# Quarter-form steps for small experts, the first of them ahead of the second half of the gather, and another order of the expert pairs

## The reference

```
logits = h @ w_router;  top_val, top_idx = top_k(logits, 2);  gate = softmax(top_val)
y[t] = sum over the token's 2 experts e of gate * (silu(h[t] @ w_gate[e]) * (h[t] @ w_up[e])) @ w_down[e]
x = x + gate_f * y;  out = rmsnorm(x, g_final)
```

## Time and profile before

| what | value |
|---|---|
| median of 3 runs | 1672.86 us (1670.66 to 1673.17) |
| profiled execution | 1672.14 us |
| its span | 1670.4 us |
| TensorE busy | 1544.0 us (92%) |
| VectorE, ScalarE busy | 418.1 us, 250.2 us |
| DMA moved | 484.43 MB, mean 290 GB/s |
| mean granted TensorE clock | 0.969 |

### The profile page before, as it was taken

The page is one execution under the profiler, slowest core; times in us unless marked ns, Lnnn a source line. Parts: engine busy times, 40 slices in busy tenths (PEclk is TensorE's granted clock), DMA queues, the critical chain, the costliest instruction groups (busy, mean ns, idle before and its releaser), DMA issues.

```text
span 1670.4 us, 21757 instructions
## 1 busy us (share of the span) xinstructions
PE 1544.0 (92%) x8696; PEld 852.4 (51%) x8697; DVE 418.1 (25%) x955; ACT 250.2 (15%) x560; POOL 0.2 (0%) x4
## 2 busy tenths in 40 slices
PE   5988889999989998599999999999999999999996
PEld 2777658777657774444444443443333443333332
DVE  2366525333344533600002000110000300003003
ACT  2132210000012331110101010011111111111112
POOL 0000000000000000000000000000000000000000
PEclk8999799999999998799999999999999999999998
DMA  9974525765656440068979797999999999997991
GB/s 348 380 266 164 189 101 192 273 252 202 227 193 229 172 178 16 1 264 332 407 289 407 284 408 294 408 374 405 408 407 407 407 377 407 407 408 296 367 377 78
DMA packets 168185, 484.43 MB, mean 290 GB/s; under 512 B 10024, under 2 KB 20544, under 8 KB 168000
## 3 DMA queue, kind: packets, MB, share of 16 engines
q1 hardware_dynamic: 168128, 483.70, 75.8%
HBM read 482.63 MB, written 1.05 MB: 290 GB/s over the span
## 4 chain that ended last, share of the span: by engine, by line
PE 79%; DMA 9%; DVE 5%; SPq 3%; ACT 2%; issue 2%; DVEq 0%; ACTq 0%
PE bank L1024 11%; PE bank L931 9%; PE bank L1064 8%; DMA ring<-in_w_exp_up 8%; PE bank L778 7%; PE bank L1008 6%; PE bank L1185 6%; PE bank L1020 5%; PE bank L949 4%; PE bank L912 4%; PE bank L1058 3%; PE bank L1211 3%; PE bank L772 3%; SPq L629 2%; PE bank L1280 2%
## 5 line engine op out<-in xcount | busy, mean ns | idle before, releaser
L1024 PE MATMUL bank<-ring,hT 128*64 128x448 f32 x1280 | 255.1, 546 | 32.2 <-DMA ring<-in_w_exp_up 12.7
L1024 PEld LDWEIGHTS bank<-ring,hT 128*64 128x64 f32 x1280 | 89.0, 137 | 190.7 <-issue 153.7
L931 PE MATMUL bank<-hT,ring 128*128 128x256 f32 x704 | 158.0, 385 | 1.7 <-DVE hT L1429 1.7
L778 PE MATMUL bank<-hT,ring 128*128 128x256 f32 x640 | 153.0, 396 | 3.9 <-ACT hT L1953 2.5
L1809 DVE TENSOR_TENSOR bt<-arena,bank 64x512 f32<-64x512 f32 (+2 forms) x36 | 24.3, 675 | 493.5 <-PE bank L1024 249.6
L931 PEld LDWEIGHTS bank<-hT,ring 128*128 128x128 f32 x704 | 135.2, 193 | 24.1 <-issue 3.8
L778 PEld LDWEIGHTS bank<-hT,ring 128*128 128x128 f32 x640 | 124.5, 198 | 26.0 <-DVE hT L1429 4.4
L1064 PE MATMUL bank<-ring,bt 128*32 128x256 f32 (+1 forms) x1232 | 136.8, 445 | 0.0
L1348 DVE SCALAR_TENSOR_TENSOR acc<-ring,cond,acc 128x512 f32<-128x512 f32 x140 | 105.2, 752 | 4.9
L1020 PE MATMUL bank<-ring,hT 128*128 128x448 f32 x256 | 100.7, 546 | 4.1 <-DMA ring<-in_w_exp_up 3.4
L1008 PE MATMUL bank<-ring,hT 128*32 128x448 f32 x1024 | 102.8, 542 | 0.0
(11 more groups left out here) (279 smaller groups left out, 1179.8 us busy)
## 6 DMA issues: line engine op xcount, KB each, us to landing
ring<-in_w_exp_gate SPq DMA_DIRECT2D x128, 896.0 KB, 9.2
ring<-in_w_exp_up SPq DMA_DIRECT2D x128, 896.0 KB, 13.0
ring<-in_w_exp_down SPq DMA_DIRECT2D x64, 1536.0 KB, 15.9
ring<-in_w_ada SPq DMA_DIRECT2D x24, 2048.0 KB, 9.4
ring<-in_w_in SPq DMA_DIRECT2D x10, 2048.0 KB, 12.8
ring<-in_w_exp_down SPq DMA_DIRECT2D x32, 512.0 KB, 16.3
ring<-in_w_ff_gate SPq DMA_DIRECT2D x5, 2048.0 KB, 12.4
ring<-in_w_ff_up SPq DMA_DIRECT2D x5, 2048.0 KB, 12.8
```

Of the source, the lines that this page charges most:

```text
L778: last = mm(o[:, 0:T], w[:, k, t * P:(t + 1) * P], hT[:, k, :], start=(k == 0), stop=(k == KC - 1))
L931: last = mm(bank[n % 2][:, a * T:(a + 1) * T], w[a][:, k, t * P:(t + 1) * P], hT[:, k, :], start=(k == 0), stop=(k == KC - 1))
L1024: last = mm(o[64 * c2:64 * c2 + 64, 64 * c2:64 * c2 + EH], xsT[:, k, t0:t0 + 64], w[:, k, c2 * EH:(c2 + 1) * EH], start=(k == 0), stop=(k ...
```

## The change

- `TINY = 32` and class 0: an expert with at most 32 tokens takes `tiny_step`, which is the quarter form alone (8 rows k of four groups), one set of transposes, and the down product in quarter form into bank 7. It waits for a gate piece and an up piece together. With the counts above, experts 0, 5 and 7 are class 0 and expert 1 stays class 1.
- `STREAM_AT` and `LONE = 1`: ranks 5, 6, 7 take positions 6, 8, 2 (before: 2, 4, 6). Round 0 has experts 0, 4, 7; round 1 (J12 to J15) is the large expert 2 alone; round 2 (J16 to J23) pairs expert 1 with expert 3, round 3 (J24 to J31) expert 5 with expert 6.
- J0 runs ahead of the second gather half, which then goes to banks 4, 5, 6, 1; the clearing of bank 7 and J0's steps on VectorE and ScalarE move with it, and `stream_weights(0)` behind it. J0 no longer waits for `yacc`; J1 does.
- More tables and branches: the flag `has_small`, the class read in each iteration, and two forms of the copy of bank 7 into `ys`.

```diff
-STREAM_AT = (0, 1, 3, 5, 7, 2, 4, 6)
-LONE = 3
+STREAM_AT = (0, 1, 3, 5, 7, 6, 8, 2)
+LONE = 1
-        small_ = {0: 2 * (s_ // 2), 1: 4, 2: 6}.get(l_)
+        small_ = {0: 2 * (s_ // 2), 2: 6, 3: 8}.get(l_)
-JOBS_DONE = [12, 20, 28, 32]
+HAS_SMALL = [int(l_ != LONE and (l_, s_) != (0, 0)) for l_ in range(4) for s_ in range(ES)]
+JOBS_DONE = [12, 16, 24, 32]
+SECOND_BANKS = (4, 5, 6, 1)
+TINY = 32
...
+            def tiny_step(J, ends):
+
+                if ends is not None:
+                    pe.wait_ge(xsS_v, ends + 1)
+                    pe.wait_ge(yacc_v, 4 * ends + 12)
+                for k in range(0, KC, 2):
+                    pe.wait_ge(full_g[k // 2], 16 * J + 16)
+                    pe.wait_ge(full_u[k // 2], 16 * J + 16)
+                    quarter(TX, range(k, k + 2), True)
+                pe.wait_ge(yzS_v, 1 if ends is None else ends + 1)
+                pe.wait_ge(eh_v, 4 * J + 4)
+                h, one_ = hs[64:P, 0, :], ident[64:P, 64:P]
+                mm(bank[3][:, 0:64], h[:, 0:P], one_, start=True, stop=True)
+                for t in range(1, 4):
+                    last = nc.tensor.transpose(bank[3][:, t * 64:(t + 1) * 64], h[:, t * P:(t + 1) * P], one_)
+                last.then_inc(et_p, 4)
+                down(J, 0, 0, ALL, (0,), 7)
...
             with pe.If(misfit == 0):
+                tiny = class_at(pe, 0)
                 pe.wait_ge(xsS_v, 1)
-                turn_scatter_weights(0, bank[3])
+                with pe.If(tiny == 0):
+                    tiny_step(0, None)
+                with pe.Else():
+                    small_step(0, None)
+                gather(1, SECOND_BANKS)
+                turn_scatter_weights(0, bank[0])
+                pe.wait_ge(sgt_a, 1)
...
-                        with pe.If(l != LONE):
-                            small_step(J, ends)
+                        partner = has_small(pe, l, i)
+                        tiny = class_at(pe, 2 * ends)
+                        with pe.If(partner == 1):
+                            with pe.If(tiny == 0):
+                                tiny_step(J, ends)
+                            with pe.Else():
+                                small_step(J, ends)
...
             with ve.If(misfit == 0):
-                stream_weights(0)
+                tiny = class_at(ve, 0)
                 gathered(0)
                 small_window(None)
+                nc.vector.memset(bank[7][:, :], 0.0).then_inc(yzS_v, 1)
+                with ve.If(tiny == 0):
+                    stream_step(0, 0)
+                with ve.Else():
+                    stream_step(0, 1)
+                stream_weights(0)
                 gathered(1)
                 large_window(1)
-                ve.wait_ge(sgt_p, 1)
-                stream_weights(1)
                 signal(nc.vector.memset(ys, 0.0), dv)
                 nc.vector.tensor_copy(yacc, xs[:, :, :]).then_inc(yacc_v, 4 * NE + 1 - 20)
                 for i in (4, 5, 6):
                     last = nc.vector.memset(bank[i][:, :], 0.0)
                 last.then_inc(yzL_v, 1)
-                ve.wait_ge(sgt_a, 1)
-                nc.vector.memset(bank[7][:, :], 0.0).then_inc(yzS_v, 1)
+                ve.wait_ge(sgt_p, 1)
+                stream_weights(1)
```

More of the change, by code:

```diff
@@ L972, in _, with gather @@
             mm(bank[1][:, 2 * NE:3 * NE], ones, chosen[:, 1, :], start=False, stop=True).then_inc(r_p, 1)
-            for h in range(2):
+            def gather(h, banks):
                 pe.wait_ge(sel_v, 2 + h)
@@ L981, in _ @@
                         last.then_inc(gat_p, 1)
+            gather(0, range(4))
             def hidden(r, J, n, i, a, unit, c=0):
@@ L1002, in hidden, with quarter @@
                         last.then_inc((eg_p, eu_p)[a], 3 if n == 1 else before_last(n, i))
-            def quarter(t0, ks):
+            def quarter(t0, ks, alone=False):
                 for k in ks:
@@ L1011, in quarter @@
                             last.then_inc(u_used if q == 3 else g_used, 1)
+                        elif alone and k == KC - 2 and q % 2:
+                            last.then_inc(eu_p if q == 3 else eg_p, 3)
             def stream_hidden(J, n, i, a, t0, c=0):
@@ L1177, in up_parts @@
                 for part_, (lo, hi) in enumerate(((0, SPLIT), (SPLIT, EH))):
-                    if part_:
+                    if part_ and ends is not None:
                         pe.wait_ge(yacc_v, 4 * ends + 12)
@@ L1301, in _ @@
                         with pe.If(l == 0):
-                            small_step(J + 2, ends)
+                            with pe.If(tiny == 0):
+                                tiny_step(J + 2, ends)
+                            with pe.Else():
+                                small_step(J + 2, ends)
                             with pe.If(i == 1):
@@ L1306, in _ @@
             with pe.Else():
+                gather(1, range(4, 8))
                 with nc.Fori(0, NE, engines=PE, head_slot={PE[0]: 0}) as r:
@@ L1806, in stream_step @@
                     up_ready(J, n, i)
-                    rows_, o = (slice(64, P), bank[2]) if n > 1 and i == ITEMS[n] - 1 else (slice(0, P), bank[1])
+                    rows_, o = (slice(64, P), bank[2]) if n != 1 and i == ITEMS[n] - 1 else (slice(0, P), bank[1])
                     n_ = EH if n == 3 and i < 2 else CW
@@ L1831, in stream_end @@
                         large_out(2, jobs)
-                nc.vector.tensor_copy(ys[64:P, 1, CW:D], bank[7][64:P, :]).then_inc(ys_v, 1)
+                with ve.If(class_at(ve, 2 * g) == 0):
+                    for c in (2, 3):
+                        last = nc.vector.tensor_copy(ys[64:96, 1, c * T:(c + 1) * T], bank[7][32 * c:32 * c + 32, 0:T])
+                    last.then_inc(ys_v, 1)
+                with ve.Else():
+                    nc.vector.tensor_copy(ys[64:P, 1, CW:D], bank[7][64:P, :]).then_inc(ys_v, 1)
                 small_window(2 * g + 2)
@@ L1882, in _ @@
                         with ve.If(l == 0):
-                            stream_step(J + 2, 1)
+                            with ve.If(tiny == 0):
+                                stream_step(J + 2, 0)
+                            with ve.Else():
+                                stream_step(J + 2, 1)
                             with ve.If(i == 1):
@@ L2034, in _, with gathered @@
             act(gt[:, :, 1], gt[:, :, 0], ACT.Exp).then_inc(r_a, 1)
-            for h in range(2):
+            def gathered(h, banks):
                 for g in (1, 3):
@@ L2161, in stream_end @@
                         large_out(2, jobs)
-                act(ys[64:P, 1, 0:CW], bank[7][0:64, :], ACT.Copy).then_inc(ys_a, 1)
+                with ae.If(class_at(ae, 2 * g) == 0):
+                    for c in (0, 1):
+                        ins = act(ys[64:96, 1, c * T:(c + 1) * T], bank[7][32 * c:32 * c + 32, 0:T], ACT.Copy)
+                    ins.then_inc(ys_a, 1)
+                with ae.Else():
+                    act(ys[64:P, 1, 0:CW], bank[7][0:64, :], ACT.Copy).then_inc(ys_a, 1)
                 scatter_weights_in(g + 1, bank[7])
@@ L2167, in _ @@
             with ae.If(misfit == 0):
-                scatter_weights_in(0, bank[3])
+                tiny = class_at(ae, 0)
+                with ae.If(tiny == 0):
+                    stream_step(0, 0)
+                with ae.Else():
+                    stream_step(0, 1)
+                gathered(1, SECOND_BANKS)
+                scatter_weights_in(0, bank[0])
                 with ae.Fori(0, 4) as l:
@@ L2184, in _ @@
             with ae.Else():
+                gathered(1, range(4, 8))
                 with ae.Fori(0, NE) as r:
```

47 lines of the change are left out of this document (32 added, 15 removed).

## The result

The changed kernel takes **1928.34 us** (median of 4 runs, 1925.82 to 1929.39) against 1672.09: a ratio of 1.153, 95% interval 1.151 to 1.155. The forecast was 1659. The steps became shorter and the kernel 256 us slower.

A forecast was written before the change was run, and what follows sets the result against it. DMA was taken to bound pairs and round 0, TensorE the lone expert. Start and round 0 gave 3.3 us, J11 7.4, the order with a tiny J24 4.9, less 1.9 small costs: 1659 us, range 1648 to 1671.

The forecast's parts named there:

- Small costs on the path: Extra branch and copy at three round ends 1.0 us (bounds 0 and 9), plus 0.9 for low-clock scatter products.
- DMA sets the pairs and round 0: Pairs of small and class-2 large steps have period 54.1 us, DMA-bound round 0 iterations 92.7, whatever small steps cost.
- A tiny step takes 12.4 us: Each tiny step: quarter form, SiLU, transposes and down sum to 12.4 us, 7.4 less than the half form.
- The start, 2.8 us won: J0 ahead of the second gather half starts at 697.5; J1 starts at 725.2, cold, net 2.8 us earlier.
- the second rival: Gain mostly eaten: first passages of new code cost 3.2 us at J0, J1, J11, a round end; 1665 mid-range; chance 0.20.
- J11 saves 7.4, the job behind the last round end 4.7, J0 on the way to J1 7.4: Savings from tiny steps at J11, at J24 behind the last round end, and at J0 before J1, in us.
- The order is worth nearly nothing: Lone expert second, rounds 2 and 3 after it: the order alone gives 0.2 us.
- From J10 on: End of round 0: TensorE binds from J10, J11 saves its whole 7.4 us, next round's first job starts at 1077.1.
- J31's quarter form: Last pair of round 3: reached at 1615.8, after six DMA-bound periods of 54.1 us from J19.
- the end: From J31's quarter form to the span's end: work as before, 38.95 us.
- The clock rival: Tiny steps leave TensorE idle, class-3 gate releases run at 1.2 GHz: 1709 us fully cold, 1676 at a third; chance 0.08.

The follow-up runs named there:

- e1: The whole change with TensorE's loop made compact, each form of step held once, same work and order, against the kernel before: 1671.57 us, ratio 1.0007.
- e2: The kernel before with two more copies of the small step in TensorE's inner loop that never run (136 unused products): 1913.64 us, one run.
- e4: The changed kernel without the half form behind round 0's large step, which this input never runs: 1686.03 us, one run.
- e5: As e1, but J0 back behind both gather halves and the copy into yacc: 1665.58 us, 0.998 of the kernel before.
- e6: As e1 with TINY = 0, so all small experts take the half form: 1689.23 us, 1.0113 of the kernel before.
- e7: As e5, but the large expert without a partner last again: 1669.07 us, 0.999 of the kernel before.
- e9: As e5, but the class-3 step does the quarter form's first six rows k between rows of the second up item: 1667.04 us, 0.9975 of before.

## Why the prediction was wrong

**The step that failed** is "Small costs on the path": 1.0 us, with bounds 0 and 9, where 257 us were measured (the changed kernel less e1). It priced one more branch at 0.37 us, a row of VectorE, and 3 us where code is passed for the first time, both per place and once. TensorE's loop, which grew by 128 products and transpositions, has no term in the sum. The mechanism left out is that the added code is part of a loop. The earlier trace rows did show such a wait (3.17 us of issue before J2), and I read it as a price of first passages that goes away. It went away in the old kernel, which fetches 3 packets from 840 us on. With some 530 instructions more in the body it does not: the price is paid in every pass, before nearly every step. e2 shows that unused code does this without any of the change, e1 and e4 that the change is rid of it with the same or nearly the same work.

What a page states would have pointed there: the Trainium skill, "Runtime: NRT & Kernel Launch", section "Instruction fetch mechanics", gives TensorE an instruction memory of 2048 instructions, refilled in 16 KiB blocks of 256 instructions, and says that a taken branch whose target lies outside the current window of two blocks has to wait for a fetch. The packets of 16.4 KB agree, and so do the packets inside the waits. The limit measured here, between 1745 and 1817, is below the stated size; seven of the page's blocks (1792) would fit it, which is an estimate from the page's figure. The window of two blocks does not agree with a body of 1745 instructions, full of jumps, that fetches next to nothing again.

The other steps can be judged on e1, where the code fits. Its chain of waits:

```profile
725.78 4.50 issue
730.28 20.53 PE bank L1037 x48
...
781.47 5.59 issue
787.06 9.06 PE bank L1023 x62
...
839.95 7.78 PE bank L1037 x20
...
932.86 7.78 PE bank L1037 x20
...
1025.26 7.78 PE bank L1037 x20
...
1088.84 12.18 PE bank L1041 x64
...
1118.33 1.33 issue
1119.66 12.25 PE bank L1041 x64
...
1467.45 4.65 PE bank L1023 x48
...
1521.53 4.65 PE bank L1023 x48
```

- *DMA sets the pairs and round 0.* Right. The class-3 periods are 92.9 and 92.4 (predicted 92.7) though both small steps are 7 us shorter, and pairs with a tiny step take 54.1, 54.8 and 54.8 (in e5 52.7, 54.0 and 54.0).
- *A tiny step takes 12.4 us.* Right at the full clock: in e5 J11 runs from 1058.65 to 1070.82, 12.2 us.
- *The start, 2.8 us won.* Wrong, in the way of the second rival. J0 began at 693.1 (predicted 697.5). But J1 began at 730.28 instead of 725.2: 4.5 us of code loading stood open behind yacc, and 3.07 even in e5, where TensorE had not run dry before. Then J1's products took 20.53 us against 18.24 (21.34 in e5, so the idle time alone isn't the reason), and J2 found 5.6 us of loading and a low clock (9.06 against 6.0 for the same products warm). J4's last up piece came at 839.95, some 9 us behind the forecast and 5.9 behind the old kernel. In e5, with J0 behind yacc, J1 starts at 724.78 and that piece comes at 834.67, within 0.6 us of the old kernel.
- *J11 saves 7.4, the job behind the last round end 4.7, J0 on the way to J1 7.4.* Right in sum: 19.5 against the 17.7 by which e6 is slower than e1.
- *The order is worth nearly nothing.* Right within what the runs can tell.
- *From J10 on.* J10 to J12 took 63.6 us, predicted 60.6, since J11's down products (4.96 against 3.27 in e5) and the scatter (8.76 against 7.13) ran at a lower clock, 0.81 to 0.85; in e5, at 1.00, the stretch took 60.3; a lone job takes 30.9, not 30.2, with 1.3 us of issue for the jump over the small forms (0.74 before). J31's quarter form came 15.2 us late in all, and the end was 3.3 us shorter than summed: 1668.6 against 1656.7.
- *The clock rival.* It gave the right sign, for a cause that did not act: after J4's last up piece the next gate load goes out 16.5 us later in e5 (851.18 - 834.67), no longer than before. The low clock of the changed kernel, 0.883 in the mean, comes from the waits for code: e1 has the same tiny steps and 0.962.

The range (1648 to 1671) held e5 and e7, versions of the change whose code fits, and missed e1, the whole change, by 0.6 us; the kernel that was asked about lies 257 us above it. What stays open is how the fetching chooses what to drop, and so why the cost per packet is 1.5 to 3.5 us and why 1817 instructions cost less than 1835. The instruction counts are approximate, and all runs are of one loop, so whether the limit is the same for another loop is not shown. Of the versions run, e5 is 0.2% faster than the kernel before; e9 has the same time within the intervals.

## What to carry to other kernels

Before costing a change to a loop, count the instructions of its body on each engine, skipped branches included: here a body of up to 1745 was nearly free (0.3%), 1817 cost 32 us and 2110 cost 243. "Issue" on the busiest engine together with a grown count of instruction packets inside its waits is the sign of it. And shortening a step beside a DMA-bound period gives back only what stands at round ends, here 18 of 89 us.

## What the runs showed of the hardware that I had not expected

- Code that never runs costs 243 us in e2, when it lengthens a loop body from about 1557 to about 2110 instructions.
- The edge is sharp: 32 instruction packets at about 1745 instructions, 41 at 1817, 60 at 1835, 148 at 2110.
- A wait for code at a first passage was 3 to 5.6 us, a chain of jumps in one lone pass 23.6 us with seven packets of 16.4 KB in it, and 1.3 us remained for a long jump inside a body that fits.
